# Seven block products for eight in the second block's gates, branch outputs and output projection, and the residual's turns moved into other waits

## What is computed

```
h = rms_norm(x, norm_mix_g)
proj = h @ w_in                         # queries, keys, values, gates
... three kinds of attention over q, k, v ...
o_a, o_b = heads' outputs, 512 wide each
gate_a, gate_b = split(sigmoid(g_merge), 2)
mix = (gate_a * (o_a @ w_a) + gate_b * (o_b @ w_b)) @ w_o
x = x + mix
x = x + hier_moe(rms_norm(x, norm_ffn_g), ...)   # 32 experts, 2 for each token
return rms_norm(x, norm_final_g)
```

## Time and profile before

| | us |
|---|---|
| median of 3 runs | 3281.34 |
| profiled execution | 3281.95 |
| its span | 3279.3 |
| TensorE busy | 3074.3 (94%) |
| VectorE busy | 1312.4 (40%) |
| ScalarE busy | 467.6 (14%) |
| POOL busy | 315.4 (10%) |

### The profile page before, as it was taken

One profiled execution on the slowest core, in us unless ns is written; L12 is line 12 of the kernel. 1 busy time (PEld: TensorE's weight loads), 2 busy tenths in 40 slices (PEclk: granted clock), 3 DMA queues, 4 the chain that ended last, 5 costly groups with the idle time before them and its releaser, 6 DMA issues.

```text
span 3279.3 us, 31761 instructions
## 1 busy us (share of the span) xinstructions
PE 3074.3 (94%) x12978; PEld 2145.1 (65%) x12978; DVE 1312.4 (40%) x2883; ACT 467.6 (14%) x1028; POOL 315.4 (10%) x304
## 2 busy tenths in 40 slices
PE   9999999979999999999998899999999989997775
PEld 7886445837888848888853568888646554453231
DVE  6563311526554335554358545553330451121112
ACT  1101010011001020000030310010211560011001
POOL 0000100210000100000101410001010570011010
PEclk9999999689999999999999999999999999988998
DMA  5222212012222212222211022222114102226997
GB/s 200 79 89 72 108 73 81 14 43 80 90 90 90 90 64 90 90 90 90 90 55 64 1 84 100 80 90 91 63 64 167 39 1 77 77 96 256 376 397 304
DMA packets 54196, 344.31 MB, mean 105 GB/s; under 512 B 7968, under 2 KB 8096, under 8 KB 15520
## 3 DMA queue, kind: packets, MB, share of 16 engines
q1 hardware_dynamic: 44352, 318.79, 26.1%
q10 hardware_dynamic: 5088, 15.06, 1.2%
q0 software_dynamic: 4608, 8.40, 0.7%
HBM read 335.92 MB, written 14.68 MB: 107 GB/s over the span
## 4 chain that ended last, share of the span: by engine, by line
PE 85%; DMA 6%; DVE 6%; ACT 2%; issue 1%; SPq 1%; POOL 0%; ACTq 0%; DVEq 0%; POOLq 0%
PE bank L805 45%; PE bank L472 24%; DMA ring<-in_weights 5%; PE bank L481 4%; PE bank L2471 2%; PE bank L1439 2%; PE bank L502 1%; PE bank L1691 1%; PE bank L508 1%; PE bank L1466 1%; DVE area L1736 1%; PE bank L1675 1%; DVE area L1988 1%; DVE area L1716 1%; DVE stat L1988 1%
## 5 line engine op out<-in xcount | busy, mean ns | idle before, releaser
L472 PE MATMUL bank<-area,ring 128*128 128x512 f32 (+1 forms) x1220 | 446.6, 527 | 21.2 <-DVE area L1569 15.6
L472 PEld LDWEIGHTS bank<-area,ring 128*128 128x128 f32 x1220 | 212.6, 192 | 250.9 <-issue 229.5
L805 PE MATMUL bank<-buf_a,mixed 128*128 128x256 f32 x1408 | 319.9, 380 | 0.0
L805 PE MATMUL bank<-buf_b,mixed 128*128 128x256 f32 x1408 | 319.3, 380 | 0.0
L805 PEld LDWEIGHTS bank<-buf_a,mixed 128*128 128x128 f32 x1408 | 268.5, 191 | 36.0 <-DVE mixed L835 0.4
L805 PEld LDWEIGHTS bank<-buf_b,mixed 128*128 128x128 f32 x1408 | 268.4, 191 | 35.5
L472 PE MATMUL bank<-buf_b,ring 128*128 128x512 f32 x656 | 285.1, 593 | 0.0
L827 DVE TENSOR_TENSOR mixed<-ring 128x512 f32<-128x512 f32 (+1 forms) x124 | 84.1, 678 | 461.1 <-PE bank L805 454.6
L805 PE MATMUL bank<-buf_a,ring 128*128 128x256 f32 x1056 | 244.6, 382 | 7.8 <-DMA buf_a<-in_x 7.3
L805 PE MATMUL bank<-buf_b,ring 128*128 128x256 f32 x1056 | 242.4, 380 | 0.4 <-ACT buf_b L696 0.4
L805 PE MATMUL bank<-area,mixed 128*128 128x256 f32 x1056 | 233.8, 380 | 0.0
(11 more groups left out here) (353 smaller groups left out, 3073.5 us busy)
## 6 DMA issues: line engine op xcount, KB each, us to landing
ring<-in_weights SPq DMA_DIRECT2D x300, 1024.0 KB, 4.8
area<-chosen SPq DMA_DIRECT2D x8, 512.0 KB, 6.8
buf_a<-in_x ACTq DMA_DIRECT2D x4, 512.0 KB, 7.6
turn_tables<-area ACTq DMA_DIRECT2D x4, 512.0 KB, 2.6
area<-turn_tables ACTq DMA_DIRECT2D x4, 512.0 KB, 4.6
tokens<-area ACTq DMA_DIRECT2D x4, 512.0 KB, 3.5
out<-area ACTq DMA_DIRECT2D x4, 512.0 KB, 2.6
const<-in_const ACTq DMA_DIRECT2D x1, 1502.0 KB, 13.6
```

The costliest lines, as they stand in the source:

```text
L472: mm = pe.e.matmul(bank[0:w.shape[1], 0:n], w, x[k], start=k == 0, stop=k == len(pieces) - 1)
L805: mm = pe.e.matmul(b, w[:, k * P:(k + 1) * P], x(INPUT_OF[p], unit.lo + k), start=(unit.key, BANK_OF[p]) not in begun, stop=unit.last and ...
```

## The change

Names of the added parts: `MERGED` lists 16 units (ga, gb, pa, pb for each of 4 pairs of output chunks), followed by 4 units "out". ga and gb have four input pairs (28 matmuls of 256 columns), pa and pb two (14), out four (28). `h_quarters`, `O_QUARTERS` and `MIX_QUARTERS` are the inputs' quarters and sums, made by VectorE: those of `h` before the attention, those of the heads' outputs after it, those of the mix once each pair of chunks is made. The first two parts of three out units are made ahead of the rest (`B_LEAD = 3`), with the last input pair held back to the end.

```diff
-SQUARE = (..., "ffn1_down", "ffn2_down", "ffn3_down")
+SQUARE = (..., "ffn1_down", "ffn2_down", "ffn3_down",
+          "b_merge", "b_out")
...
+        plan["b_merge"] += (square(*w[:2], out, halves, cols=merge_columns(BM)) + square(*w[:2], out, halves, cols=merge_columns(BM + D)) +
+                            square("w_a_2", (0,), out, fours, pair_rows) + square("w_b_2", (0,), out, fours, pair_rows))
...
-LATE = {st: 2 if st in ("ffn1", "ffn2", "ffn3") else 1 for st in STATS}
+LATE = {st: 2 if st in ("ffn1", "ffn2", "ffn3", "nsa") else 1 for st in STATS}
...
-    BESIDE, IDLE_ROOT, IDLE_SCALE, IDLE_RMS = ("ffn1", "ffn3"), 6, 6, 3
+    BESIDE, IDLE_ROOT, IDLE_SCALE, IDLE_RMS = ("ffn1", "ffn3", "nsa"), 6, 6, 3
...
+            if beside and n % 2:          # scalar_ln
+                beside(ac, n // 2)
...
     def tensor_nsa(pe, stream, h, ready):
-        for m in range(KD):
-            product(pe, stream, g, ("ga", m), plan["b_merge"][4 * m], x)
-            ...
+        for way, c in MERGED:
+            unit = unit_of[("square", "b", way, c), 0]
+            if way in ("ga", "gb"):
+                tensor_parts(pe, unit, PARTS, lambda name, k: quarters[k][name], lambda name, k: b_mixed("h", k))
+            else:
+                lo = 2 * (way == "pb")
+                tensor_parts(pe, unit, PARTS, lambda name, k: O_QUARTERS[lo + k][name], lambda name, k: b_mixed("o", lo + k))
+        ...
+        for unit in leading:
+            for p in (1, 2):
+                tensor_part(pe, unit, p, mixed_x, range(KD // 2 - 1), mixed_at)
+        for unit in leading:
+            for p in (1, 2):
+                end(g, tensor_part(pe, unit, p, mixed_x, (KD // 2 - 1,), mixed_at), (unit.key, 0, p))
+        for c, key in enumerate(B_KEYS[len(MERGED):]):
+            tensor_parts(pe, unit_of[key, 0], PARTS[2:] if c < B_LEAD else PARTS, mixed_x, mixed_at)
...
     def scalar_nsa(ac, st, r):
+        for way, c in MERGED:
+            copy_first(way, c)
+            if way in ("ga", "gb"):
+                ac.wait_ge(*read_of(("square", "b", way, c))[3])
+                ac.e.activation(merged[way], merged[way], ACT.Sigmoid).then_inc(gate_sig, 1)
...
     def vector_nsa(ve, h, r):
+        for c in range(KD // 2):
+            for way in ("ga", "gb", "pa", "pb"):
+                collect(way, c)           # as in the FFN's up half
+            ...
+            ve.step(tt(merged["ga"], merged["ga"], merged["pa"], ALU.mult))
+            ve.step(tt(merged["gb"], merged["gb"], merged["pb"], ALU.mult))
+            ve.settle()
+            ve.step(tt(n_mix[:, 2 * c + 1, :], merged["ga"][:, 0:T], merged["gb"][:, 0:T], ALU.add))
+            ve.step(tt(n_mix[:, 2 * c, :], merged["ga"][:, T:2 * T], merged["gb"][:, T:2 * T], ALU.add))
+            ve.settle()
+            vector_mix_inputs(ve, MIX_QUARTERS[c], MIX_QUARTERS[c]).then_inc(x_mixed, 1)
...
+    XT_ROOT, XT_SCALE, XT_RANK = (0, 1), (2,), (3,)
     def scalar_route(ac, before):
         ac.e.dma_start(gain, io["gain"]).then_inc(gain_loaded, 16)
+        scalar_turn_half(ac, "xt", xt, xt_done, 0, 0)
+        scalar_rms_sqrt(ac, "nsa")
+        scalar_turn_half(ac, "xt", xt, xt_done, 0, 1)
+        scalar_turn_tokens(ac, "xt", xt, xt_done, (1, 2))
+        rows(0)                           # two copies and the store of one block of tokens
         ac.wait_ge(route_diff, 1)
         ac.e.activation(ge, ge, ACT.Exp).then_inc(route_exp, 1)
+        rows(1)
         ac.wait_ge(route_diff, 2)
         ac.e.activation(r_w[:, :, 1:2], r_m, ACT.Exp).then_inc(route_exp, 1)
+        rows(2)
+        rows(3)
+        scalar_turn_tokens(ac, "xt", xt, xt_done, XT_RANK)
...
-        scalar_ple_proj(ac, 1, 0)
-        scalar_ln(ac, "ffn3", buf_a, buf_b, 5 * KD)
-        scalar_ple_proj(ac, 1, KD // 2)
+        scalar_ple_proj(ac, 1, range(KD // 2))
+        scalar_ln(ac, "ffn3", buf_a, buf_b, 5 * KD, lambda e, n: scalar_ple_proj(e, 1, (KD // 2 + n,)))
```

More of the change, by code:

```diff
@@ L89, in square @@
             for out, side in ((first, 0), (second, 0), (first, 1), (second, 1)):
-                pieces += [(name, index, ((pair[side] * P, P),), ((out * P, P),)) for pair in ins[lo:lo + GROUP]]
+                pieces += [(name, index, rows(pair[side]), cols(out)) for pair in ins[lo:lo + GROUP]]
         products.append(pieces)
@@ L1100, in tensor_ple_proj, with scalar_ple_proj @@
             product(pe, stream, g, ("proj", layer, m), plan[f"ple{layer}_proj"][m], cols(pt))
[L1102 to L1103 removed]
+    def scalar_ple_proj(ac, layer, ms):
+        for m in ms:
             ac.wait_ge(*g.done(("proj", layer, m)))
@@ L2250, in build_in, with plan_turned_tokens @@
     r_m, e_in, r_w = place(276, 1), place(288, EPG), chunks(weight, TB)
+    XT_ROOT, XT_SCALE, XT_RANK = (0, 1), (2,), (3,)
+    def plan_turned_tokens(name, done, bs):
+        for b in bs:
+            for half in range(2):
+                g.add((name, b, half), (done, 2 * b + half + 1))
     def plan_route():
+        plan_turned_tokens("xt", xt_done, XT_SCALE)
         for b in range(TB):
```

249 lines of the change are left out of this document (168 added, 81 removed).

## The result

The changed kernel takes 3233.24 us, median of 4 runs (3226.69 to 3239.90), against 3281.51 us of the kernel before on the same chip (4 runs, 3281.14 to 3282.65). The ratio is 0.9852, 95% interval 0.9832 to 0.9873, so 48.6 us faster (the medians differ by 48.3; 43.0 was the forecast, from 3281.34 to 3238.7). The measured median lies at the low end of the range of 3233 to 3248; on the prediction's base of 3281.34 us the ratio gives 3232.8, 0.2 us outside. The interval there is 3226.2 to 3239.7 and reaches into the range, so the time alone says little about which term was wrong; the traces say it. The profiled execution is the fastest of the four: 3226.69 us, span 3224.6.

The account below looks back on a forecast made before the run. TensorE's own time was taken to bound the kernel almost everywhere. Terms -27.9 + 0.2 + 1.7 + 0.6 - 2.6 - 14.6 = -42.6 took 3281.95 to 3239.35, less 0.61 is 3238.7 us; range 3233 to 3248.

Parts of the forecast that it names:

- Merge -27.9: Merge and output projection: 896 records of 256 columns replace 512 of 512 columns, 193.9 us for 221.8.
- the clock's rival: Rival: TensorE's clock falls in the new merge form; 3297 us at 30% at the lower clock; chance 0.02.
- the hand-overs': Rival: weights or banks come late in the short pa and pb units; +11, 3250 us; chance 0.07.
- Embedding's copies -14.6: Two ple norms: TensorE's lead no longer waits for ScalarE's later copies behind all eight outputs, and runs at full clock.
- Last norm +0.2 and +1.7: Last out unit's fold ends 0.2 us later; a residual copy ahead of the root's table load adds 1.7.
- The 32 turns behind the table: 0: Behind the slot table: removing the turns frees no time, as TensorE waits there for gathered rows until 2971.12.
- Clock in the router +0.6: Router: its 64 records take 12.0 us instead of 11.41 if the clock is low from the start.
- Routing -2.6: Router to ranks: an earlier exponential lets ranks start 2.6 us earlier, then limited by TensorE's eight residual transposes.

Follow-up runs that it names:

- the turns put back: Changed kernel with all 32 residual turns and their copies back behind the slot table, idle products of the last norm back too: 3230.83 us, ratio 0.9851.
- the turns alone moved: Kernel before with the residual's 32 turns moved ahead of root, router and ranks, plus VectorE's share of the last norm's sums as changed: 3274.54 us, 0.9976.
- taking away that wait alone: Changed kernel with all 32 turns behind the slot table, TensorE's branch no longer waiting for ScalarE's last copy of them: 3237.88 us, one run.
- the exponentials alone: Kernel before with only the two exponentials moved, behind ScalarE's second and fourth copies of the normed rows: 3273.97 us, ratio 0.9975.
- The embedding's copies alone: Kernel before with only ScalarE's copies of the embedding's projection put between its outputs of the norm: 3268.22 us, ratio 0.9963.

## Why the prediction came out as it did

- **Merge -27.9: right**, -27.80, at a mean clock of 1.00 in all three traces of the changed kernel. Neither the clock's rival nor the hand-overs' showed there. In 3 of the 11 traces with the new form the stage took 1.0 to 2.5 us more because it began at 0.50, but there the attention's last 4 us already ran at 0.50, and within 6 us of the new products the clock was at 1.00: it is what the attention left and not a fall in the new form. The Trainium skill's page "TensorE: Matmul & The Clock Gate", section "A second HAM failure mode: psum-queue depth-cycling", was cited for that rival: a clock that goes down and up while a kernel goes round its PSUM banks. The traces do not bear that out in this stretch: behind its first 10 us the clock is at 1.00 in all 11.
- **Embedding's copies -14.6: right**, -14.75, and the wait was the one named. (The working as written, 7.4 + 7.3 less 0.1 twice, gives 14.5.)
- **Last norm +0.2 and +1.7: right**, +0.25 and +1.81.
- **"The 32 turns behind the table: 0": this is the step that failed.** It took the stretch 2958.88 to 2971.12 for a wait for the gathered rows because their issue at 2960.97 lay in it. The row said otherwise: the wait ahead of the first expert turn was put down to "issue", and the gather landed at 2965.3. What ended last was turns, copies, the wait for the last copy, and 5.3 us up to the first expert turn, with the branch in them. The stretch from table to turn came out 4.80 us shorter where the term has 0; the turns put back cost 4.2 us there, the turns alone moved take 5.3 away (11.05 to 5.77), and taking away that wait alone gives 3.5.
- **Clock in the router +0.6: wrong in sign**, -1.54 here; 8.96 to 11.50 us over the traces of kernels with the new merge. I assumed it low from the start. It was 1.00 over the router's first 3.0 us and 0.84 over the next 2.0, where the kernel before had 0.97 over its first 2.84 us, and 0.50 behind that in both. What decides it isn't settled.
- **Routing -2.6: right in what is late next** (the turns ahead of the ranks), short by 0.9, mostly because those turns ran at 1.00: the ranks started 0.87 us behind their start, for the 1.5 assumed. **The ranks' own 2.9 us were in no term.** I moved their start and kept their length; with no idle time ahead of them they run at the full clock, as the exponentials alone show (2.32 us for 4.45, and 8.01 for 11.38 up to the table).
- **The attention's +1.04 was in no term.** The embedding's copies alone, with the attention's code as before, give +1.07 there: it is the earlier arrival and another course of the clock, and not the sums for `h` that VectorE now makes in it.

Sum of what was missed: -4.8 -2.9 -2.1 -0.9 +1.0 = -9.7, which brings -42.6 to -52.3, where the table has -52.1 between head and experts. The medians show 47 to 49. The table's traces make the change look larger than the medians do, since two of the three traces of the changed kernel are the fastest of its 13 runs. Its three traces differ by over 1 us only in the head (1157.4 to 1159.2) and the experts' stretch (304.9 to 315.5), so the 3.5 us most likely lie there; the runs without a trace can't show it.

## What to carry to other kernels

Where the profile puts a wait down to "issue", nothing that you can name ended it: don't put a transfer in its place because one lies in the same stretch, but work out when that transfer was done. In these traces TensorE's first product behind a branch on a value came 5.05 to 5.35 us after the last wait ahead of it, and 2.77 us behind the work already issued where no open wait stood between: keep such waits out from ahead of a branch. When an instruction moves up to where TensorE hasn't idled, its length changes too, here from 4.45 to 2.32 us for 20 small products. And a change that gains 3 us in one stretch has to be shown in that stretch, when runs of one kernel lie 13 us apart.

## What the runs showed of the hardware that I had not expected

- TensorE's branch: 5.05 to 5.35 us over seven traces from the end of the last copy, which it waits for, to the first product, whether or not the flag is read ahead; 2.77 us from the last product's end when that wait is gone, and instruction packets on the DMA queues in it.
- The same attention code takes 309.5 to 315.4 us by how long the clock stands at the lower level. The four traces with the earliest head (1156.1 to 1157.1 us) have the dearest stretch of attention and merge, 3.6 to 5.2 us over what 531.9 and the merge's -27.8 would give; all with a head of 1157.2 us or later lie between -0.7 and +1.7. That is a hint, not a finding.
- The experts' stretch spreads over 13 us, 303.2 to 316.2. TensorE's waits for weights in it range from 40.2 us (303.2) to 52.0 (316.2), and follow it only in part: 47.1 at 315.5, 46.9 at 308.2.
